# A feed-forward's norm by token halves, with GpSimd making the first ordinary pair's weight sums

## What is computed

```python
def conv_ffn(h, w_up, conv_w, conv_b, w_down):          # first block's feed-forward, D_FF = 2816
    a, b = jnp.split(h @ w_up, 2, axis=-1)
    ac = conv_b + sum(conv_w[i] * a_pad[:, i:i + S] for i in range(CONV_W))
    return (jax.nn.gelu(ac) * b) @ w_down
x = x + conv_ffn(rmsnorm(x, norm_ffn[l]), w_up[l], conv_w[l], conv_b[l], w_down[l])
x = rmsnorm(x, norm_final)                              # end of the first block
h = modulate(rms_norm(x), sh_m, sc_m)                   # second block: h * (1 + scale) + shift
proj = h @ w_in[l]
...
h = modulate(rms_norm(x), sh_f, sc_f)
ffn = (jax.nn.silu(h @ ffn_w_gate[l]) * (h @ ffn_w_up[l])) @ ffn_w_down[l]
```

## Time and profile before

| | |
|---|---|
| median of 3 runs | 3486.67 us (3484.3 to 3486.73) |
| the profiled execution | 3486.89 us |
| its span, first to last instruction | 3485.1 us |
| TensorE busy | 3257.6 us, 93% |
| VectorE busy | 1998.3 us, 57% |
| ScalarE busy | 1230.9 us, 35% |
| GpSimd busy | 894.3 us, 26% |
| mean granted TensorE clock | 0.962 of full speed |

### The profile page before, as it was taken

The page is one execution under the profiler, slowest core; times in us unless marked ns, Lnnn a source line. Parts: engine busy times, 40 slices in busy tenths (PEclk is TensorE's granted clock), DMA queues, the critical chain, the costliest instruction groups (busy, mean ns, idle before and its releaser), DMA issues. The chain is left out here.

```text
span 3485.1 us, 56038 instructions
## 1 busy us (share of the span) xinstructions
PE 3257.6 (93%) x22553; PEld 2688.7 (77%) x22553; DVE 1998.3 (57%) x3144; ACT 1230.9 (35%) x2077; POOL 894.3 (26%) x502
## 2 busy tenths in 40 slices
PE   8999999999998988999999899979988979999999
PEld 7888888877887777777778777768776758888887
DVE  5852556533876567777778526144433365555685
ACT  3111222122665134444345520235432143333443
POOL 2332333346110532222200144132221332222000
PEclk9999999999999999999999999979997989999999
DMA  4454434334001424444374365220010313323742
GB/s 127 139 186 128 122 109 122 112 113 136 9 9 58 136 70 136 147 146 161 117 266 133 97 170 128 91 98 22 21 39 10 126 55 121 106 91 103 262 133 97
DMA packets 355294, 387.95 MB, mean 111 GB/s; under 512 B 27328, under 2 KB 258290, under 8 KB 353834
## 3 DMA queue, kind: packets, MB, share of 16 engines
q1 hardware_dynamic: 327518, 303.89, 28.3%
q10 hardware_dynamic: 26560, 78.27, 5.9%
q0 software_dynamic: 960, 2.21, 0.3%
HBM read 271.98 MB, written 112.33 MB: 110 GB/s over the span
## 5 line engine op out<-in xcount | busy, mean ns | idle before, releaser
L1104 PE MATMUL bk<-ffn_bhi,ffn_ahi 128*128 128x512 f32 x1240 | 491.6, 401 | 61.9 <-ACT ffn_u L1317 33.4
L1104 PE MATMUL bk<-ffn_blo,ffn_ahi 128*128 128x512 f32 x1240 | 486.1, 396 | 0.0
L1104 PE MATMUL bk<-ffn_bhi,ffn_alo 128*128 128x512 f32 x1240 | 486.1, 396 | 0.0
L1070 POOL TENSOR_TENSOR ffn_alo<-ffn_raw,ffn_ahi 128x512 fp32r<-128x512 f32 x134 | 217.3, 1632 | 718.7 <-ACT ffn_ahi L1248 718.7
L223 PE MATMUL acc<-h_hi,whi 128*128 128x512 f32 x1136 | 373.4, 408 | 23.4 <-DVE h_lo L2803 6.7
L223 PE MATMUL acc<-h_lo,whi 128*128 128x512 f32 x1136 | 357.8, 394 | 0.0
L223 PE MATMUL acc<-h_hi,wlo 128*128 128x512 f32 x1136 | 356.1, 393 | 0.0
L206 POOL TENSOR_TENSOR whi<-raw,ones 128x1024 fp32r<-128x1024 f32 (+1 forms) x83 | 157.2, 1894 | 745.1 <-PE acc L223 552.9
L1104 PEld LDWEIGHTS bk<-ffn_bhi,ffn_ahi 128*128 128x128 f32 x1240 | 238.1, 192 | 125.4 <-issue 69.9
L1104 PEld LDWEIGHTS bk<-ffn_bhi,ffn_alo 128*128 128x128 f32 x1240 | 237.7, 192 | 51.5
L1104 PEld LDWEIGHTS bk<-ffn_blo,ffn_ahi 128*128 128x128 f32 x1240 | 238.9, 193 | 49.4
(11 more groups left out here) (601 smaller groups left out, 6467.3 us busy)
## 6 DMA issues: line engine op xcount, KB each, us to landing
ffn_graw<-ffn_gated SPq DMA_DIRECT2D x154, 256.0 KB, 2.7
raw<-w_in SPq DMA_DIRECT2D x51, 512.0 KB, 4.0
projT<-proj_stage ACTq DMA_DIRECT2D x51, 512.0 KB, 3.0
ffn_ada_raw<-w_ada SPq DMA_DIRECT2D x12, 2048.0 KB, 9.0
ffn_raw<-w_up SPq DMA_DIRECT2D x44, 512.0 KB, 6.7
ffn_gated<-ffn_gout SPq DMA_DIRECT2D x44, 512.0 KB, 3.3
ffn_gated<-ffn_gt SPq DMA_DIRECT2D x22, 768.0 KB, 6.2
ffn_drow<-w_down SPq DMA_DIRECT2D x44, 256.0 KB, 5.6
```

What stands on the lines that cost most here:

```text
L1070: nc.gpsimd.tensor_tensor(a_lo[:, slot], source, a_hi[:, slot], ALU.subtract).then_inc(s[f"low{slot}"], 1)
L1104: ins = nc.tensor.matmul(o, wt[:, w, k, :], xt[:, x, k, :], start=first and i == 0, stop=last and i == 2, skip_group_check=reopened)
```

## The change

In both heads of the feed-forwards and in the projections' head the steps are half tiles, 512 tokens of one k. In the feed-forward the order is k 0 to 3 of half 0, k 0 to 3 of half 1, then k 4 to 7 in the same way (`FIRST_ORDER`, steps n = 0 to 15); VectorE starts when its half's factors are spread. TensorE takes six matmuls for a step. VectorE makes low parts of even n, GpSimd of odd n. T1 is made in two pieces of 2 tiles, after steps 9 and 11 (`make_t1`). GpSimd, and no longer VectorE, makes S1, S2 and S4 of pair 1 (`first_sums`), the low part of S1 and S2 (`first_low_sums`) and the low part of T3. ScalarE makes the high parts of two of the four first weight parts after step 3 and not ahead of step 0 (`second_high`), those of S1 and S2 after step 10 and that of T1 after step 13. In the projections the order is all k of half 0, then all k of half 1, `mid` is four half buffers in the same room, and each half of the factors has its own signal. An unused class and function are deleted.

```diff
@@ TensorE, pair 0
-                for k in range(KD):
+                for n, (k, t) in enumerate(FIRST_ORDER):
...
-                    pe.wait_ge(s["b_low_p"] if k % 2 else s["b_low_v"], k // 2 + 1)
-                    xs = (A11_B11, A22_T4) if k < 4 else (A12_B21, S4_B22)
+                    pe.wait_ge(s["b_low_p"] if n % 2 else s["b_low_v"], n // 2 + 1)
                     for out, w in ((a0, A11_B11 if k < 4 else A12_B21), (b0, S4_B22 if k < 4 else A22_T4)):
-                        last = passes([out[:, 0, :], out[:, 1, :]], w, xs, k % 4, k == 0, k == KD - 1)
+                        last = passes([out[:, t, :]], w, [b_slot(k, t)], k % 4, k == 0, k == KD - 1)
@@ GpSimd
+            def first_sums():
+                pool.wait_ge(s["raw_in1"], 32)
+                pool_steps.link(nc.gpsimd.tensor_tensor(a_sum[:, S1_T1], part(1, 1, 0), part(1, 1, 1), ALU.add))
+                nc.gpsimd.tensor_tensor(a_sum[:, S2_T2], a_sum[:, S1_T1], part(1, 0, 0), ALU.subtract).then_inc(s["s12_made"], 1)
+                pool.wait_ge(s["s12_made"], 1)
+                nc.gpsimd.tensor_tensor(s4[:], part(1, 0, 1), a_sum[:, S2_T2], ALU.subtract).then_inc(s["s4_made"], 1)
+            def first_low_sums():
+                pool.wait_ge(s["high1"], 1)
+                pool.wait_ge(s["s4_made"], 1)
+                nc.gpsimd.tensor_tensor(a_lo[:, S1_T1:S2_T2 + 1], a_sum[:, S1_T1:S2_T2 + 1], a_hi[:, S1_T1:S2_T2 + 1],
+                                        ALU.subtract).then_inc(s["low1"], 1)
             low(A11_B11, part(0, 0, 0), 1)
             low(S4_B22, part(0, 1, 0), 1)
+            low_b(1)
+            low_b(3)
             low(A12_B21, part(0, 0, 1), 1)
             low(A22_T4, part(0, 1, 1), 1)
-            for k in range(1, KD, 2):
...
+            low_b(5)
+            low_b(7)
+            first_sums()
+            low_b(9)
+            low_b(11)
+            low_b(13)
+            first_low_sums()
+            low_b(15)
             low(A11_B11, part(1, 0, 0), 2)
             low(A12_B21, part(1, 0, 1), 2)
+            pool.wait_ge(s["t_high"], 3)
+            nc.gpsimd.tensor_tensor(b_lo[:, S3_T3], T3, b_hi[:, S3_T3], ALU.subtract).then_inc(s["t3_low"], 1)
             low(A22_T4, part(1, 1, 1), 2)
             low(A11_B11, part(2, 0, 0), 3)
@@ ScalarE
-            for k in range(KD):
-                act.wait_ge(s["mid_done"], k + 1)
+            for n, (k, t) in enumerate(FIRST_ORDER):
+                act.wait_ge(s["mid_done"], n + 1)
+                x = h[:, k, cols(t)]
...
+                nc.scalar.activation(b_hi[:, b_slot(k, t), k % 4, :], x, ACT.Copy).then_inc(s["b_high"], 1)
+                if n == 3:
+                    second_high()
+                if n == 10:
+                    high_sums(1)
+                if n == 13:
+                    high_t(S1_T1, T1, "t1_made", 2)
             high_11(1)
-            high_t(S1_T1, T1, "t1_made")
             high_12(1)
-            high_sums(1)
             high_t(S2_T2, T2, "t2_made")
@@ VectorE
-                dve.wait_ge(s["rstd_done"], 2)
-                for k in range(KD):
+                for n, (k, t) in enumerate(FIRST_ORDER):
+                    if n in (0, 4):
+                        dve.wait_ge(s["rstd_done"], t + 1)
...
-                    if k % 2:
-                        low_b(k - 1)
+                    if n % 2:
+                        low_b(n - 1)
+                    if n in (9, 11):
+                        make_t1(n // 2 - 4)
...
+            def make_t1(j):
+                two = slice(2 * j, 2 * j + 2)
+                dve.wait_ge(s["b_high"], 6 + 2 * j)
+                dve.wait_ge(s["b_low_p"], j + 1)
+                dve.wait_ge(s["b_low_v"], j + 1)
+                tt(T1[:, two], quarter[0][1][:, two], quarter[0][0][:, two], ALU.subtract).then_inc(s["t1_made"], 1)
...
             norm_and_low()
-            make_t1_t3_t2()
-            make_s1_s2_s4(1)
             low_t(S1_T1, T1, 1)
-            low_s1_s2(1)
+            make_t3_t2()
+            make_s3(1)
             low_t(S2_T2, T2, 2)
-            dve.wait_ge(s["t_high"], 3)
-            tt(b_lo[:, S3_T3], T3, b_hi[:, S3_T3], ALU.subtract).then_inc(s["t3_low"], 1)
-            make_s3(1)
             low_s3(1)
             convolve(0)
             make_t4()
@@ TwoNorms, VectorE
-            dve.wait_ge(s["rstd_done"], 1)
-            for k in range(KD):
...
+            for n, (k, c) in enumerate(self.steps):
+                if n % KD == 0:
+                    dve.wait_ge(s["rstd_done"], n // KD + 1)
+                if n == 2:
...
+                if n >= 5:
+                    dve.wait_ge(s["lo_done"], n - 4)
+                nc.vector.scalar_tensor_tensor(out=mid[n % 4][:], in0=xT[:, k, c], scalar=prm[:, gain + k:gain + k + 1],
+                                               in1=both_rstd[:, c], op0=ALU.mult, op1=ALU.mult).then_inc(s["mid_done"], 1)
@@ projections, TensorE
-            for k in range(KD):
-                norm.ready(pe, k)
-                for b in range(2):
-                    last = tile_products(nc, acc[b], w_hi[b], w_lo[b], hi, lo, k, KD)
+            for t in range(NH):
+                for k in range(KD):
+                    norm.ready(pe, t * KD + k)
+                    for b in range(2):
+                        last = half_products(nc, acc[b], w_hi[b], w_lo[b], hi, lo, k, KD, t)
```

More of the change, by code:

```diff
@@ L216, in three_pass, with half_products @@
     return last
+def half_products(nc, acc, w_hi, w_lo, hi, lo, k, k_tiles, t):
+    for i, (w, x) in enumerate(((w_hi, hi), (w_hi, lo), (w_lo, hi))):
+        last = nc.tensor.matmul(acc[:, t, :], w[:, k, :], x[:, k, t * HALF:(t + 1) * HALF],
+                                start=(k == 0 and i == 0), stop=(k == k_tiles - 1 and i == 2))
+    return last
 def tile_products(nc, acc, w_hi, w_lo, hi, lo, k, k_tiles, w_cols=slice(0, P), halves=NH):
@@ L520, in pool_part @@
+        self.steps = [(k, slice(t * HALF, (t + 1) * HALF)) for t in range(NH) for k in range(KD)]
     def pool_part(self, pool):
         nc, hi, lo = self.nc, self.env["hi"], self.env["lo"]
-        for k in range(1, KD):
-            pool.wait_ge(self.s["hi_done"], k + 1)
-            nc.gpsimd.tensor_tensor(lo[:, k, :], self.mid[k % 2][:], hi[:, k, :], ALU.subtract).then_inc(self.s["lo_done"], 1)
-    def ready(self, pe, k):
-        if k == 0:
+        for n, (k, c) in enumerate(self.steps[1:], 1):
+            pool.wait_ge(self.s["hi_done"], n + 1)
+            nc.gpsimd.tensor_tensor(lo[:, k, c], self.mid[n % 4][:], hi[:, k, c], ALU.subtract).then_inc(self.s["lo_done"], 1)
@@ L542, in programs @@
         diag = self.mem.at(f"{name}_diag", at, [P, 2 * NT, P])
-        self.mid = mid = [self.mem.at(f"{name}_mid{b}", at + 16 + 4 * b, [P, S]) for b in range(2)]
+        self.mid = mid = [self.mem.at(f"{name}_mid{b}", at + 16 + 2 * b, [P, HALF]) for b in range(4)]
         both_rstd, first_rstd = (x.rearrange("p h t -> p (h t)") for x in (tot, other))
@@ L557, in _ @@
                     pe.wait_ge(s["diag_done"], (j * NH + h + 1) * NT // 2)
-                    last = nc.tensor.matmul(out[:, h, :], ones[:], diag[:, tile:tile + NT // 2, :], start=True, stop=True)
-                last.then_inc(s["rstd_done"], 1)
+                    nc.tensor.matmul(out[:, h, :], ones[:], diag[:, tile:tile + NT // 2, :], start=True, stop=True).then_inc(s["rstd_done"], 1)
         @block.scalar
@@ L959, in feed_forward @@
         spare = 3
-        halves = lambda k: slice(A11_B11, A22_T4 + 1, 5) if k < 4 else slice(A12_B21, S4_B22 + 1, 3)
+        b_slot = lambda k, t: ((A11_B11, A22_T4), (A12_B21, S4_B22))[k // 4][t]
+        FIRST_ORDER = [(4 * r + k, t) for r in range(2) for t in range(2) for k in range(4)]
+        cols = lambda t: slice(t * HALF, (t + 1) * HALF)
         quarter = [[h[:, 4 * r:4 * r + 4, t * HALF:(t + 1) * HALF] for t in range(2)] for r in range(2)]
@@ L4322, in _ @@
                 pe.wait_ge(s[f"weight_split{b}"], 1)
-            for k in range(KD):
-                norm.ready(pe, k)
-                for b in range(2):
-                    last = tile_products(nc, acc[b], w_hi[b], w_lo[b], hi, lo, k, KD)
-                    if k == KD - 1:
-                        last.then_inc(s[f"products_done{b}"], 1)
+            for t in range(NH):
[3 more added lines that the diff above has]
+                        last = half_products(nc, acc[b], w_hi[b], w_lo[b], hi, lo, k, KD, t)
+                        if k == KD - 1 and t == NH - 1:
+                            last.then_inc(s[f"products_done{b}"], 1)
             for u in range(2, N):
```

172 lines of the change are left out of this document (43 added, 129 removed).

## The result

| | before | after |
|---|---|---|
| median | 3487.42 us (9 runs, 3482.86 to 3494.28) | 3496.69 us (9 runs, 3494.9 to 3508.39) |
| profiled execution, span | 3486.89, 3485.1 | 3496.11, 3494.3 |

After is slower: the ratio is 1.0031, with a 95% interval of 1.0018 to 1.0044, so 6 to 15 us. Forecast were 3490.5 (+3.7 on its base; "within 0.2%" was the likeliest case). The median lies inside the range of 3477 to 3498, beyond the 0.2%.

The account below looks back on a forecast made before the run. TensorE, busy 93% of the span, was taken as the bound, with VectorE's chain deciding the first feed-forward's head. Projections -5.1, first feed-forward +6.8 and second +2.0 summed to +3.7, giving 3490.5 us, range 3477 to 3498.

Parts of the forecast that it names:

- within 0.2%: Whole kernel: time indistinguishable from no change, about 7 us either way; chance 0.56.
- Paid in TensorE's two waits: First feed-forward's head: the 6.8 us loss shows in the two waits TensorE already had there.
- What counts is VectorE's chain, not how soon TensorE began: First feed-forward's head, kernel before: VectorE, almost without pause from 1279.17, sets the end of TensorE's second wait, near 1318.
- Loss 2.0: Second feed-forward's head: T4's low part ends at 2860.5 instead of 2858.49, 2.0 us lost.
- ScalarE ends its halves at 2834.6: Second feed-forward's head: ScalarE modulates sixteen half steps at 1.27 us each, sums and high parts between, ending at 2834.6.
- same tail as above: Second feed-forward's head: work behind the first pair runs as in the first feed-forward, putting T3's low part at 2852.4.
- The earlier start finds full clock: First feed-forward's head: TensorE, starting 3.3 us earlier, avoids the reduced clock; with the start, 5 us if unhindered.
- still at half clock: Second feed-forward's head: TensorE starts at 2808.5 instead of 2812.45, but at half clock.
- GpSimd asks first: Rival, feed-forward heads: GpSimd wins close turns and its weight parts delay T4's low part; about 7 us more, 3497; chance 0.13.
- 1.8 us more work: Feed-forward heads: GpSimd gains 1.8 us more work than VectorE loses, an argument for the rival at 3497.
- Half steps pay in full: Rival, all three heads: without turn-taking they gain -8.4, -5.1 and the projections' share, -18.6 together, 3468; chance 0.17.

Follow-up runs that it names:

- m_turns: Separate kernel computing nothing of the reference: eight pairings of VectorE and GpSimd instructions started together, three times each; GpSimd's 2048 elements took 4.49 us alone, 4.91 when waiting.
- e_proj: Kernel before with only the new TwoNorms and the projections' loop over halves; ratio 0.9991 [0.9980, 1.0002].
- e_halves: Changed kernel with the weight sums and T3's low part back on VectorE, T1 whole, orders behind the halves as before; one run, heads 60.48, 33.82, 64.05 us.

## Why the prediction was right and wrong

**Turns: right.** The argument that GpSimd and VectorE take turns by whole instructions, from the stretched rows, was shown by m_turns and by the rows above. It forecast S3's low part at over 4 us (4.65), T3's low part at 4.7 (4.58; the Trainium skill's 4497 ns, GPSIMD Engine Reference, section 3.1, is what m_turns measured without a neighbour, 4.49) and low halves of over 1.2 (1.92 in the row). TensorE's waits for low halves were forecast at 1 to 3 us and were 1.28 and 0.75, with 1.40 for a weight part. The Trainium skill, GPSIMD Engine Reference, section 1 (Specifications), names contention with VectorE work in a 2-port perf mode or on two SBUF inputs. The prediction took up the second kind only; the tensor_scalar of m_turns has one input, runs 1024 elements in 0.69, the time of an addition of 512, and held GpSimd as well (4.91 against 4.49 alone).

**Head 1: the size right, the chain read in part.** +6.8 was forecast, +5.9 measured. T4's low part was forecast at 1317.0, 58.35 after the start, and ended at 57.53. "Paid in TensorE's two waits" does not fit: they grew by 0.5 and 1.6, and the rest are new waits ahead of them. "What counts is VectorE's chain, not how soon TensorE began" was half true of the kernel before: VectorE's chain there waits for ScalarE, which waits 6.50 for TensorE's first pair, and in e_proj 1.1 us more of that lengthened the head by 1.1.

**The projections: nearly right.** -5.1 forecast, -4.26 measured. The prediction has 1.28 for ScalarE's half step; the rows show 1.37, since the modulation of 512 elements takes 0.80, and not 0.71, for which the prediction gives no row. Over sixteen half steps that is 1.4 us. The last low part of x ended 27.05 after the spreading, where TensorE's last step was forecast to begin at 26.55; GpSimd's split, forecast to end at 31.85, ended at 32.62, and TensorE restarted 1.13 behind it, as forecast.

**Head 2: the term that failed.** "Loss 2.0" measured +4.64. Its step "ScalarE ends its halves at 2834.6" used 1.27 for each of sixteen half steps; 1.37 make 1.6 more, and the last half ended at 2840.01, which less the later start of 3.65 is 2836.4, 1.8 late. The "same tail as above" then had one turn more: T3's and T2's additions both took 3.37. T3's low part ended 2.6 later than forecast, and the 2.6 are still there at the end. This is arithmetic on the rows of one trace; no run tests ScalarE's pace by itself.

**TensorE's clock: wrong in both heads.** "The earlier start finds full clock" did not hold in head 1: the clock was 0.50 until 1270. In head 2, where "still at half clock" was forecast, it was full. What this cost or gave no run tells.

**The verdict: one step too mild.** "Within 0.2%" failed because head 2 was 2.6 and the projections 0.8 dearer than forecast and head 1 only 0.9 cheaper: +6.3 in place of +3.7. That is itself just under the 7 us that I called indistinguishable. What carried the measurement beyond it, 2.9 in the two traces and 2.0 by the fit, lies outside the heads; the prediction put it at nothing, and its cause stays open. That 3496.69 still lies inside the stated range owes something to the rival at its upper end, whose mechanism did not happen. The rival "GpSimd asks first" (3497) came out nearest in time: GpSimd's weight parts did not come between T4 and its low part, which took 2.29 in both heads, and which way the close turns fell is not known. Its "1.8 us more work" for GpSimd is too small by the prediction's own prices: 3 x 1.16 + 2.35 + 4.7 = 10.5 against 5.6 makes 4.9. "Half steps pay in full" fell with e_halves: with nothing moved to GpSimd the halves lengthen head 2 by 1.6 and gain nothing in head 1.

## What to carry to other kernels

Before VectorE's work goes to GpSimd, look at what VectorE does in that stretch. Behind a GpSimd instruction of 4.58 us a VectorE operation of 0.69 on SBUF inputs took 4.65; VectorE instructions that read PSUM kept their 1.28 beside one of 4.61. Halving the steps started TensorE 3.0 to 3.6 us sooner in all three heads. It paid in the projections, where what TensorE waits for next follows the steps' end; e_proj changed the halves, the four buffers and the signal for each half together, so what each is worth is not shown. It did not pay in the feed-forwards, where a chain of VectorE and ScalarE comes last and the halves give both more instructions and more turns. A piece of work pulled forward can move TensorE's stop, and with it the half clock that follows, onto the chain that others wait for. And when the same code takes 1.1 us more in another run, follow the wait back before calling it noise: here it was TensorE's clock at the first products, passed on through ScalarE.
